# Weight products of a 2-layer hybrid encoder on one core: each of the three fp32r products for both column halves in turn

## The reference, cut to what matters

```python
def swiglu(h, w_gate, w_up, w_down):
    return (jax.nn.silu(h @ w_gate) * (h @ w_up)) @ w_down

h = modulate(x, w['norm_pre'][l, slot], mod[:, slot, 0], mod[:, slot, 1])
y = swiglu(h, w['ffn_w_gate'][l, j], w['ffn_w_up'][l, j], w['ffn_w_down'][l, j])   # four of these
z = h @ w['ab_w_in']     # and o @ w['ab_w_out'], h @ w['gdn_w_in'], o @ w['gdn_w_out']
```

## Time and profile before

| | us |
|---|---|
| median of 3 runs | 3967.85 |
| lowest, highest run | 3966.62, 3967.96 |
| span of the profiled execution, first to last instruction | 3966.7 |
| TensorE matmuls busy, in the span | 3697.3 (93%) |
| TensorE weight loads busy | 3441.6 (87%) |
| GpSimd busy | 2197.0 (55%) |
| VectorE busy | 1991.0 (50%) |
| ScalarE busy | 580.2 (15%) |

### The profile page before, as it was taken

The page is one execution under the profiler, slowest core; times in us unless marked ns, Lnnn a source line. Parts: engine busy times, 40 slices in busy tenths (PEclk is TensorE's granted clock), DMA queues, the critical chain, the costliest instruction groups (busy, mean ns, idle before and its releaser), DMA issues.

```text
span 3966.7 us, 63424 instructions
## 1 busy us (share of the span) xinstructions
PE 3697.3 (93%) x26506; PEld 3441.6 (87%) x26506; DVE 1991.0 (50%) x2200; ACT 580.2 (15%) x1157; POOL 2197.0 (55%) x956
## 2 busy tenths in 40 slices
PE   6999999899999899999899999989889997999997
PEld 3999999778567899999789999978878777999997
DVE  5734636549533737356553443566765335322334
ACT  2000000321332200000210000042132123000001
POOL 3767767556003567667666777756600005777775
PEclk9999999899789999999899999989999658999998
DMA  5333323243001324223122232212300001222221
GB/s 204 136 108 111 136 101 118 78 107 131 7 22 43 106 97 144 106 106 140 64 95 101 105 113 100 101 56 75 79 9 1 1 1 54 85 87 93 85 85 65
DMA packets 80752, 342.75 MB, mean 86 GB/s; under 512 B 13960, under 2 KB 17544, under 8 KB 50936
## 3 DMA queue, kind: packets, MB, share of 16 engines
q1 hardware_dynamic: 36976, 248.02, 17.6%
q10 hardware_dynamic: 43656, 93.04, 7.3%
HBM read 329.93 MB, written 11.11 MB: 86 GB/s over the span
## 4 chain that ended last, share of the span: by engine, by line
PE 74%; issue 12%; POOL 6%; DVE 5%; ACT 2%; ACTq 1%; POOLq 0%; DVEq 0%
PE psum L578 61%; POOL w_lo L494 3%; POOL w_hi L491 2%; PE psum L562 2%; DVE arena L1532 1%; PE psum L1001 1%; PE psum L983 1%; PE psum L943 1%; PE psum L955 1%; PE psum L1004 1%; PE psum L1002 1%; PE psum L958 1%; ACTq L1141 1%; PE psum L545 1%; PE psum L616 1%
## 5 line engine op out<-in xcount | busy, mean ns | idle before, releaser
L491 POOL TENSOR_TENSOR w_hi<-raw,one_col 128x1024 fp32r<-128x1024 f32 x464 | 934.7, 2014 | 1682.9 <-PE psum L600 829.4
L578 PE MATMUL psum<-h_hi,w_hi 128*128 128x272 f32 x5120 | 1489.5, 291 | 21.9 <-POOL w_lo L494 16.1
L578 PE MATMUL psum<-h_hi,w_lo 128*128 128x272 f32 x5120 | 1481.5, 289 | 0.0
L578 PE MATMUL psum<-h_lo,w_hi 128*128 128x272 f32 x5120 | 1477.8, 289 | 0.0
L494 POOL TENSOR_TENSOR w_lo<-raw,w_hi 128x1024 fp32r<-128x1024 f32 x464 | 1221.2, 2632 | 36.4
L578 PEld LDWEIGHTS psum<-h_hi,w_hi 128*128 128x128 f32 x5120 | 965.2, 189 | 43.1 <-issue 42.0
L578 PEld LDWEIGHTS psum<-h_lo,w_hi 128*128 128x128 f32 x5120 | 965.4, 189 | 0.2 <-issue 0.2
L578 PEld LDWEIGHTS psum<-h_hi,w_lo 128*128 128x128 f32 x5120 | 964.5, 188 | 0.0
L578 PE MATMUL psum<-hid_hi,w_hi 128*128 128x272 f32 x2048 | 607.4, 297 | 0.6
L578 PE MATMUL psum<-hid_hi,w_lo 128*128 128x272 f32 x2048 | 600.1, 293 | 0.0
L578 PE MATMUL psum<-hid_lo,w_hi 128*128 128x272 f32 x2048 | 598.0, 292 | 0.0
(11 more groups left out here) (284 smaller groups left out, 3328.3 us busy)
## 6 DMA issues: line engine op xcount, KB each, us to landing
raw<-in_w_stream SPq DMA_DIRECT2D x232, 1024.0 KB, 4.8
arena<-in_ada_w ACTq DMA_DIRECT2D x72, 768.0 KB, 5.6
arena<-in_ada_w ACTq DMA_DIRECT2D x32, 384.0 KB, 4.3
spare<-in_ada_w ACTq DMA_DIRECT2D x5, 768.0 KB, 16.9
rel_spread<-arena ACTq DMA_DIRECT2D x1, 3072.0 KB
spare_h<-in_ada_w ACTq DMA_DIRECT2D x3, 768.0 KB, 15.7
x<-in_x_t SPq DMA_DIRECT2D x1, 2176.0 KB, 18.6
out_y_t<-x SPq DMA_DIRECT2D x1, 2176.0 KB, 7.0
```

What stands on the lines that cost most here:

```text
L491: pool.tensor_tensor(w_hi[:, u], raw[:, s, u], one_col[:].broadcast_to([P, D]), ALU.mult)\
L578: mm = pe.matmul(psum[:, 2 * u + b, 0:HT], a[:, u, w], m[:, k, t], start=(k == 0 and i == 0), stop=(k == KD - 1 and i == 2))
```

## The change

For each contraction tile the loop over the three products is now outside and the loop over the two column halves inside, in both functions that make weight products. Each product goes to the first half's bank and then to the second half's, then the next product follows. The stationary tile thus stays the same for four matmuls (w_hi) and then for two (w_lo).

```diff
@@ unit @@
-                    for b in range(2):
-                        w = slice(k * P, (k + 1) * P)
-                        t = slice(b * HT, (b + 1) * HT)
-                        for i, (a, m) in enumerate(((w_hi, hi), (w_hi, lo), (w_lo, hi))):
-                            mm = pe.matmul(psum[:, 2 * u + b, 0:HT], a[:, u, w], m[:, k, t],
+                    w = slice(k * P, (k + 1) * P)
+                    for i, (a, m) in enumerate(((w_hi, hi), (w_hi, lo), (w_lo, hi))):
+                        for b in range(2):
+                            mm = pe.matmul(psum[:, 2 * u + b, 0:HT], a[:, u, w], m[:, k, b * HT:(b + 1) * HT],
                                            start=(k == 0 and i == 0), stop=(k == KD - 1 and i == 2))
```

## The result

| | before | after |
|---|---|---|
| median of 8 runs, us | 3967.75 | 3957.74 |
| lowest to highest | 3966.17 to 3975.66 | 3953.47 to 3958.85 |
| span of the profiled execution | 3966.7 | 3957.0 |

The ratio is 0.9972, with a 95% interval from 0.9962 to 0.9982. So the change makes the kernel faster by 10.0 us between the medians, 0.28% by the ratio: a little more than the 0.2% that the prediction takes as what a measurement can tell from no change.

A forecast was written before the change was run, and what follows sets the result against it. The prediction took TensorE's chain of weight products, spaced 0.1263 us start to start, to bound the kernel. Its terms, 0 + 0 + 0 us on the 3966.7 us span, left the median unchanged at 3967.8 us, range 3947 to 3989.

The forecast's parts named there:

- no-change case: Whole kernel: the order does not move the spacing, median stays 3967.8 us, within 3960 to 3976; chance 0.69.
- Sensitivity: Weight products on TensorE's chain, about 19,100 matmuls: 1 ns on every start-to-start time is worth about 19 us.
- Waits and hand-overs: Around each unit's 48 matmuls: nothing is moved past a wait and unit_done stays on the last matmul; 0 us.
- Weight loads: TensorE's stationary tiles: 26506 loads again, and a repeated tile steps like a fresh one, 127 ns each; 0 us.
- third rival: Loads of a repeated tile fall away in four steps of six: 165 us less, 3803 us; chance 0.02.
- Banks and the new pair: Weight-product steps to the other bank, also with the same tile: no dearer than others; 0 us between −42 and +42.
- three sums of three steps: Timeline piece with ten starts: three kinds of step each total 0.38 us, taken to hide at most 3.3 ns a step.
- Whatever makes 113 into 126 acts on every step alike.: Weight products: the 13.0 ns of spacing over the 113.3 ns stream of 272 columns is the same for every step.
- faster: adding twice in a row into one bank: Weight products: successive adds into one bank cost something, alternating gives rest; 3926 us, 3947 at half; chance 0.15.
- slower rival: Steps from one half to the other: every change of bank costs 3.3 ns; +42 us, 4010 us, 3989 at half; chance 0.14.
- What would show it: Last FFN's 4512 matmuls: 570 us within 2 us if right, 567 or less if faster, 573 or more if slower.

The follow-up runs named there:

- bank_only: Changed kernel with another order of the six matmuls: half and bank turn six times, stationary tile repeats in 1 step of 6; 3958.53 us, ratio to before 0.9978.
- neither: Changed kernel with another order of the six matmuls: bank changes in 2 steps of 6, stationary tile repeats in 1; 3968.08 us, ratio to before 1.0005.
- after_256: Changed kernel streaming 256 columns instead of 272 per weight product, except each unit's first in a bank; 3843.86 us in one execution.
- banks_alternate: Changed kernel with banks turning at each step but column halves streamed in before's order (not the correct linear layer); 3966.9 us in one execution.
- halves_alternate: Changed kernel with streamed column halves turning at each step but banks in before's order (not the correct linear layer); 3958.3 us in one execution.
- half_load: Changed kernel loading 64 instead of 128 stationary columns in the two correction products; 3965.69 us in one execution.
- pair_cross: Changed kernel taking two contraction tiles together, each product for both tiles on half 0, then both on half 1; 3940.18 us, ratio to before 0.9930.
- pair_rotate: Changed kernel taking two contraction tiles together, each product for both halves of one tile, then of the next; 3940.84 us, ratio to before 0.9930.

## Why the prediction was right or wrong

I forecast no change, 3967.8 us, with 0.69 on it, a range from 3947 to 3989, and 0.17 on faster. The measured 3957.7 us lies in the range, but the effect is just outside my no-change case of 3960 to 3976, on the side to which I gave 0.17. That the range holds it is due to its width, which the rivals gave it, and not to the mechanism that I forecast.

- *Sensitivity.* 19,100 matmuls on the chain, 19 us per ns. The spacing fell by 0.85 ns, which gives 16 us; 10 came. This step held in kind. It lacked that TensorE stops for GpSimd's split at two places in four units, of which the chain of the earlier trace rows shows one, and above all that the clock takes part: 17.1 us more at the half level.
- *Waits and hand-overs, 0 us.* Right in the main: the chain, its shares and the counts are the same, and TensorE's waits for w_lo add up to 0.8 us more.
- *Weight loads, 0 us.* Right: 26506 loads, and bank_only and neither show that a repeated tile is worth nothing. The third rival is refuted by the count.
- *Banks and the new pair, 0 us between −42 and +42.* **This is the step that failed.** The size was −0.85 ns per matmul. I had set it to 0 because three sums of three steps read 0.38 us each. Such a display cannot tell 3.3 ns, as I wrote, and the question was one of 0.4 ns; equal sums at that coarseness were no reason for 0.69. The bound was too narrow besides: the three steps of a sum are not neighbours, so each can be off by 10 ns by itself, and what the sums can hide is 10 ns a step and not 3.3. Rows that average over hundreds of matmuls, as those of the earlier trace rows, tell 0.01 ns, but they show one order only. None of the rows that I read could have told the sign.
- *"Whatever makes 113 into 126 acts on every step alike."* after_256 confirms an extra of about 12 ns over the stream. That it is the same in any order was wrong: it depends on the sequence of streamed addresses. The order of the halves never stood in the working as something of its own; I had only "bank" and "tile" as attributes, and the half goes with the bank in this code. The 115.8 ns beside it, from the Trainium skill, page "TensorE: Matmul & The Clock Gate", section "Back-to-back issue gap", are given there for an isolated matmul. No run here has one alone, so the 125.4 ns of this stream do not contradict it, as I had written.
- *The rival "faster: adding twice in a row into one bank".* Right in sign, and its middle value of 21 us was twice what came. Its mechanism is refuted by banks_alternate. So is the slower rival's: every matmul there changes bank, at no cost (570.03 us). The rule that I had named beside it, of the Trainium skill, page "Perfetto Trace Analysis", section "Matmul Optimizations", is to use all 8 PSUM banks for parallelism. No run here changes how many banks are used, so the rule itself is not tried; going to the other bank at each matmul brings nothing.
- *What would show it.* I had written that 567 us or less in the last FFN would speak for the faster rival, with GpSimd idle for less time; 566.2 came, and GpSimd's idle time ahead of w_hi fell from 1682.9 to 1671.7 us. These signs fit the size of the rival and not its mechanism: they could not tell bank from half. And that the spacing would have to move by over 0.4 ns for me to be wrong; it moved by 0.85.

## What to carry to other kernels

Where one matmul follows the next for most of the time, the order in which operands are streamed is worth a trial, even when no instruction, wait or byte changes: it was worth 0.7% of the spacing, and no row read from the old profile showed it. Before calling an attribute of the order irrelevant, list all that go with it (bank, stationary tile, streamed address) and take them apart. And a saving in spacing arrives only in part: price the engine that is next in line, and expect the clock's stretches to fall elsewhere. Where two engines slow each other, see which of them starts first: here that order went with some 2.2 us less waiting at each of eight places, more in all than the change of spacing brought.

## What the runs showed of the hardware that was not expected

- The time between the starts of matmuls with 272 columns depends on the start addresses of the streamed operand in SBUF: 126.3 ns with the halves in runs of three, 125.4 ns with the halves in turn (102.35 / 816), with banks and stationary tiles without influence (banks_alternate, halves_alternate, bank_only, neither).
- The same instructions at the same addresses settle on different spacings in different stretches: 101.68 and 103.48 us for 816 matmuls (124.6 and 126.8 ns).
- At full clock a matmul takes its columns plus 12 ns here (118.6 ns for 256, 125.5 ns for 272), of which a stationary tile of half the width takes nothing away.
- The granted clock fell in stretches whose instructions the change does not touch: in the delta-net mixer 163.9 us in a row at half clock in place of 153.6. One execution of a kernel with the spacing of after lost nearly all of its gain so (half_load, 3965.69 us, clock 0.932).
- A sum of VectorE (128 x 1536) took 3.4 us where GpSimd's w_hi had started 0.25 to 0.50 us before it, and 1.8 us where it started first; w_hi then took 3.2 to 3.3 us in place of 2.1 to 2.3 (after against pair_cross and pair_rotate, eight places each).
